# Three split weight buffers and eight raw ones in place of four and six

## The reference, cut to what matters

```python
for l in range(DEPTH):                                   # first block
    mod = silu_c @ w_mod[l] + b_mod[l]
    shift, scale, gate = jnp.split(mod[:, None, :], 3, axis=-1)
    h = rmsnorm(x, norm_g[l]) * (1.0 + scale) + shift
    u = h @ e_w_in[i]                                    # layer 0; o_w_in in layer 1
    ...
    y = jnp.concatenate([y1, y2], axis=-1) * jax.nn.silu(ug)
    x = x + gate * (y @ w_o[l])
...
h = rmsnorm_2(x, norm0); x = x + (y * jax.nn.silu(gate)) @ w_out   # second block, twice
```

## Time and profile before

| | |
|---|---|
| median of three runs | 2377.14 us |
| the profiled execution | 2377.5 us |
| its span, first to last instruction | 2375.7 us |
| TensorE busy (PE) | 2330.6 us, 98% |
| VectorE busy (DVE) | 1502.2 us, 63% |
| ScalarE busy (ACT) | 1040.7 us, 44% |
| weights and tokens read | 438.59 MB |
| DMA | 200 GB/s on average |
| mean granted clock of TensorE | 0.999 |

### The profile page before, as it was taken

The page is one execution under the profiler, slowest core; times in us unless marked ns, Lnnn a source line. Parts: engine busy times, 40 slices in busy tenths (PEclk is TensorE's granted clock), DMA queues, the critical chain, the costliest instruction groups (busy, mean ns, idle before and its releaser), DMA issues. The chain is left out here.

```text
span 2375.7 us, 31312 instructions
## 1 busy us (share of the span) xinstructions
PE 2330.6 (98%) x11556; PEld 1895.8 (80%) x11556; DVE 1502.2 (63%) x2508; ACT 1040.7 (44%) x1755; POOL 271.1 (11%) x403
## 2 busy tenths in 40 slices
PE   6999999999999999999999999999999999999998
PEld 1578888877778888877878889878888888998887
DVE  2288555666777887877656666675675544544655
ACT  3232333344443222524544455444454445654543
POOL 0011120111110000012121000100110001101200
PEclk9999999999999999999999999999999999999999
DMA  9978454544434756585665556765655676667653
GB/s 369 365 265 282 163 168 138 167 153 160 143 113 166 238 190 224 181 270 190 191 199 156 164 190 202 223 214 162 218 173 187 191 224 196 203 196 239 190 194 135
DMA packets 236423, 474.60 MB, mean 200 GB/s; under 512 B 18886, under 2 KB 47924, under 8 KB 235504
## 3 DMA queue, kind: packets, MB, share of 16 engines
q1 hardware_dynamic: 210768, 394.27, 51.0%
q0 software_dynamic: 25216, 77.81, 10.4%
q10 hardware_dynamic: 288, 0.52, 0.1%
HBM read 438.59 MB, written 33.94 MB: 199 GB/s over the span
## 5 line engine op out<-in xcount | busy, mean ns | idle before, releaser
L2334 PE MATMUL pp<-w_hi,hT_hi 128*128 128x512 f32 (+4 forms) x2520 | 1004.1, 398 | 1.8 <-DVE w_lo L1682 1.8
L2336 PE MATMUL pp<-w_hi,hT_lo 128*128 128x512 f32 (+4 forms) x2520 | 964.9, 383 | 0.0
L1682 DVE TENSOR_TENSOR w_lo<-raw,w_hi 128x1024 fp32r<-128x1024 f32 (+4 forms) x562 | 658.6, 1176 | 481.0 <-ACT w_hi L1379 479.4
L2335 PE MATMUL pp<-w_lo,hT_hi 128*128 128x512 f32 (+4 forms) x2520 | 962.1, 382 | 0.0
L1379 ACT ACTIVATE w_hi<-raw 128x1024 fp32r<-128x1024 f32 (+4 forms) x562 | 569.4, 1018 | 427.3 <-PE pp L2336 300.8
L2334 PEld LDWEIGHTS pp<-w_hi,hT_hi 128*128 128x128 f32 x2520 | 473.9, 188 | 100.5 <-issue 21.4
L2336 PEld LDWEIGHTS pp<-w_hi,hT_lo 128*128 128x128 f32 x2520 | 473.0, 188 | 89.5
L2335 PEld LDWEIGHTS pp<-w_lo,hT_hi 128*128 128x128 f32 x2520 | 474.5, 188 | 80.4 <-issue 4.3
L1792 DVE SCALAR_TENSOR_TENSOR arena<-raw,cT,arena 128x512 f32<-128x512 f32 x240 | 170.4, 745 | 2.1 <-DMA raw<-in_w_mod_dram 0.2
L1549 ACT ACTIVATE arena<-pY 128x512 f32<-128x512 f32 (+2 forms) x122 | 63.5, 520 | 197.9 <-PE pY L2504 192.6
L2329 PE MATMUL pp<-hT_hi,w_hi 128*128 128x512 f32 x352 | 149.6, 425 | 0.0
(11 more groups left out here) (358 smaller groups left out, 2010.7 us busy)
## 6 DMA issues: line engine op xcount, KB each, us to landing
raw<-in_w_in_dram SPq DMA_DIRECT2D x168, 512.0 KB, 4.2
raw<-in_w_mod_dram SPq DMA_DIRECT2D x153, 512.0 KB, 5.4
raw<-in_e_w_in_dram SPq DMA_DIRECT2D x90, 512.0 KB, 5.5
raw<-in_w_o_dram SPq DMA_DIRECT2D x64, 512.0 KB, 4.2
raw<-in_o_w_in_dram SPq DMA_DIRECT2D x64, 512.0 KB, 4.7
raw<-in_w_out_dram SPq DMA_DIRECT2D x64, 512.0 KB, 3.9
raw<-in_w_in_dram SPq DMA_DIRECT2D x56, 440.0 KB, 4.0
arena<-in_w_mod_dram SPq DMA_DIRECT2D x39, 512.0 KB, 11.2
```

Source lines behind the costliest of these rows:

```text
L1682: dve.tensor_tensor(w_lo[:, g.s % SPLIT, 0:n], raw_of(g)[:, 0:n], w_hi[:, g.s % SPLIT, 0:n].bitcast(F32), ALU.subtract).then_inc(lo_done, 1)
L2334: pe.matmul(dst, hT_hi[:, kk, o:o + P], hi[:, k, :], start=a, stop=False)
L2335: pe.matmul(dst, hT_hi[:, kk, o:o + P], lo[:, k, :], start=False, stop=False)
L2336: ins = pe.matmul(dst, hT_lo[:, kk, o:o + P], hi[:, k, :], start=False, stop=z)
```

## The change

One of four split buffers is given up, and two raw buffers are added. A split buffer is w_hi and w_lo of a group, 8 KB for each partition, a raw buffer 4 KB, so the memory is the same. Both numbers go into more than the sizes of the tensors: RAW into the ring of the raw buffers (L159), SPLIT into the slot of every split (L148), into the wait of ScalarE's split (L1377) and, by split_at, into the places of the side groups in the list of loads (L285).

```diff
-RAW = 6
+RAW = 8
 MORE = 7
-SPLIT = 4
+SPLIT = 3
 AHEAD = 3
 EARLY = 5
 LEAD = 3
```

## The result

The changed kernel takes 2400.34 us (median of four runs, 2396.05 to 2401.12) against 2376.95 us for the kernel before on the same chip: a ratio of 1.0094, interval 1.0082 to 1.0106. The prediction was 2383 with a range of 2375 to 2390. The profiled execution of the changed kernel is its shortest one, 2396.05 us with a span of 2394.2, so a trace of it accounts for 18.5 us of span and not for 23.4; what the other three executions have more than it, 4 to 5 us, no trace here shows.

What follows compares the result with a forecast made beforehand. TensorE, busy for 98% of the span, was taken as the bound. Terms -1.0 + 5.7 + 1.8 + 1.4 - 1.2 - 1.0 = +5.7 us took the profiled 2377.5 to 2383.2, predicted as 2383, range 2375 to 2390.

Steps and rivals of the forecast that it cites:

- What bounds the kernel: Whole run: TensorE is busy for 98% of the span, so buffers can only change the little that it waits.
- Raw buffers, the start: Start, bound by DMA: the deeper ring mends the 1.22 us wait at 93.69 us; -1.0 us, ends 0 and -1.8.
- Raw buffers after the start: After the start: late raw loads make ScalarE wait, but TensorE has its next groups split; 0, ends 0 and -1.8.
- rival "faster": Whole run: the deeper ring decides and waits on ScalarE's results go; about -5.5, 2372 us, chance 0.10.
- The plain lead: Undisturbed two-quanta groups: w_lo's spare time falls from 5.8 to 3.1 us with the gate one group later, costing nothing.
- (c): Chunks idx0 and idx1: a split moves behind ScalarE's squares, so w_lo comes later; +1.8 us, ends 0 and +3.
- (f): Mixer c and chunks c_q1 and d_q: first head zero net, the heads after it gain; -1.0 us, ends -2.5 and +3.
- (a): Mixer a, first units of eight heads: the split now stands between exp and probabilities, 0.25 us late each; +2.0 us.
- (b): Mixer a, head 4's third unit and the next, beside the gate chunk: +2.8 us; head 6 repeats it: +0.9.
- (d): Heads of e and f: splits before max or after exp; e's last two lose 0.7 and 0.3, f +0.4; sum +1.4.
- (e): Heads of h with an odd slot: the split in front of max goes behind exp; -1.2 us, ends 0 and -1.3.
- rival "much slower": Wherever VectorE is over 3.1 us behind: three buffers are too few and stalls spread; 2394 us, chance 0.07.

Runs made afterwards that it cites:

- best_places: Changed kernel (three split, eight raw buffers) with splits of mixers a and b, out0_0 to out0_3, y1_0 to y1_3 and from e0 on one slot later: 2375.76 us.
- e0: Not a run: the chunk of the kernel from which the splits of layers 2 and 3 are counted; no time of its own.
- e1: Not a run: a chunk of the kernel in stage e, where TensorE waits for w_lo; no time of its own.
- order3_buf4: Kernel before, with four split and six raw buffers kept, but each split at the place that three buffers give it: 2395.67 us.
- raw6_split3: Changed kernel with six raw buffers in place of eight, still three split buffers: 2405.38 us.

## Why the prediction was wrong, point by point

**What bounds the kernel.** Right: TensorE's busy time stayed and every loss is a wait of TensorE.

**Raw buffers, the start, -1.0.** Right in sign and place: -1.6 in stage b, the wait at 93.69 us and the dip are gone. Not all of it is the ring's: with six raw buffers and the new list of loads, four traces still have 0.2 to 1.2 us of that wait, and behind it they lie between 1.1 us ahead of the kernel before and 0.4 behind it.

**Raw buffers after the start, 0 with ends 0 and -1.8.** Mis-sized. They are worth 4.1 us there (5.2 less 1.1) in the order of best_places, and 8.1 by the traces in the changed kernel's own order. The reason given, that TensorE has its next groups split already when a load is late, holds for w_lo in an undisturbed stretch; it left out that ScalarE and VectorE, standing at a load, are late with everything behind it, as in d, and that side groups which come late hold TensorE at mod_cols, as in o0. The prediction had that argument in its rival "faster" and gave it 0.10. The rule named there from the Trainium skill (DMA: Bandwidth & Descriptors, Rules for kernel authors), to issue a DMA early and wait late, agrees with this part: the deeper ring, by which loads go out earlier, won 5.0 and 5.3 us at two orders.

**The plain lead, 5.8 us down to 3.1, costing nothing undisturbed.** Right where it was claimed, o1, o2 and o3 have no loss over 0.1 us. But "this cover goes where ScalarE or VectorE is behind" was priced in (c) and (f) alone; the fourth buffer by itself, with six raw ones, was worth 9.7 us (8.8 by the traces), of which 4.3 in e and 3.0 in o0, two stages that the sum did not have under this head. What it looks like in e1 of the changed kernel, VectorE and TensorE:

```profile
1513.99 0.69 DVE L1950 TENSOR_TENSOR arena<-xy,arena 128x512 f32<-128x512 f32 x1 [1.86 <-DMA arena<-scratch_u]
...
1521.08 1.22 DVE L1682 TENSOR_TENSOR w_lo<-raw,w_hi 128x1024 fp32r<-128x1024 f32 x1
...
1522.35 0.50 PE L2334 MATMUL pp<-w_hi,hT_hi 128*128 128x512 f32 x1 [1.75 <-DVE w_lo L1682]
```

VectorE stood 1.86 us for a transfer, works without a break from there, and the split comes in its turn, 1.75 us late. With four buffers and the same order (order3_buf4) e loses nothing.

**(a) and (b), mixer a, +5.7.** The mechanism was right, the size short: 7.9 in the stages, 8.8 in mixer a itself, since 0.9 was won in mixer b. The waits at 622.06, 631.03 and 687.08 (1.63, 1.77, 1.63) and the smaller one for mod_cols, 0.42 for 1.55, are as worked out; head 4 gives 2.7 where 2.8 was said. First units cost 0.3 each in seven heads, where 0.25 was said, and 1.0 in the first head. Not seen were two waits for ScalarE's copy L1589, 1.08 us at 562.84 and 0.75 at 693.37, which stands behind the moved split as well.

**(c) idx, +1.8.** Right sign, half the size: 0.9.

**(d) e and f, +1.4.** This is the step that failed. Measured 9.8: e 2.1, f 3.5, y2 4.2. Three parts of it went wrong. Mixer f (y2) was put at +0.4 and cost 4.2. The text had the chain "exp, split, split, probabilities adds 2.2" for mixer a and did not carry it to f, which makes its probabilities in the same way. It let f "gain and lose in turn", since the parity of the slots alternates, but the two turns don't cancel: the heads with the better place won back waits of 0.14 to 0.30 us, and those with the worse place, whose chain grew by 2.09 in the one shown above, waited 1.08, 1.66 and 1.23. Mixer e (stage f) was put at +1.0 for its last two heads, which cost 1.4 together, so that this mechanism was right; its first head was not looked at and cost another 1.7, at its exp and at the transposes of the next head's queries (L2456). And chunk e1 had no term: there the late w_lo just shown cost 2.1. The runs also part (d) by cause: with four split buffers in the same order (order3_buf4, six raw ones) it is 3.8, e 0.0, f 1.6 and y2 2.2. So the place alone makes 3.8. The smaller cover of three buffers, which the sum had at nothing in these stages, adds 8.2 at six raw buffers (raw6_split3: 4.3, 3.5 and 4.2), and the two raw buffers take 2.2 of it back, in e.

**(e) h, -1.2.** Half right. The waits at 2245.20 us and its like are gone, -0.9 in y3; but 0.7 came back in h by L2211, a step of mixer g. Mixer g had no term: its split went between two steps of its chain and cost 1.8. Nor had y1, where VectorE's rope (L1921) stands behind a moved split: 1.1 in its stage.

**(f) c and d, -1.0.** Right, -1.4 (1.3 and -2.7): the wait of 1.73 us at the first head of c went, and a wait for w_lo came.

In sum: of the 12.9 us between 5.7 and the 18.6 of the traces, 8.4 are (d), 2.2 the stages of mixer a, 2.9 mixer g and y1, which were not looked at, and 1.1 (e); the other terms take 1.7 back. The 4 to 5 us by which the median lies above the trace stay open. By cause instead of by stage, the forecast had -1.0 for the raw buffers, nothing of its own for the lost split buffer and +6.7 for (a) to (f), the places; measured were -5.0, +9.7 and +18.2. So the places are the largest miss, and two more misses, of 4.0 and 9.7, offset each other in part by luck. The rival "much slower" gave the nearest number, 2394, by another mechanism: stalls that spread because three buffers are too few. Its own part, the buffer, was 9.7 us; the larger part, 18.2, needs no buffer taken away. The most doubtful term was said to be (b); it was among the best worked out, with mixer a's waits at the times that it named.

## What to carry to other kernels

Where a constant sets both a ring's size and the place of its work in a hand-written order, change them apart: here the same memory was 23 us slower or 2.8 us faster with nothing but the slots of the splits between, and 18 entries of the list of loads that follow them. In a bound engine's supply, gains and losses of a move don't average: go through every chain that the move enters, since a chain with slack gives nothing back. What a buffer is worth depends on the order too: the fourth split buffer was worth 9.7 us at one set of places and, by estimate, about nothing at another. And place work that waits at a gate behind the gate, and behind the step of the chain that shares its slot.

## What the runs showed of the hardware that was not expected

The four executions of the changed kernel lie 5.1 us apart (2396.05 to 2401.12), at a granted clock of 0.997 to 0.998, and the four of the kernel before beside them 1.0 (2376.57 to 2377.52). That is no difference between the kernels by itself: 22 later executions of the kernel before lie 4.6 us apart (2375.14 to 2379.71). The clock doesn't sort them either, since the changed kernel's shortest and longest executions both had 0.998. What makes executions differ is open. The two kernels that mended its places each gained 4 us more in the medians than in the traces, which fits a profiled execution of the changed kernel that was 4 us short of its usual time.
